# Half of an output projection, for two of four superblocks, moved beside the first four attention blocks of a hybrid decoder layer

## The reference, cut to what matters

```python
att_out = dsa_attention(q, k, v, qi, ki, wi)          # [B, T, 512]
hg_out = hgrn2_mixer(hq, hf, hi, hg, ...)             # [B, T, 512]
mix = jnp.einsum('bte,ed->btd', jnp.concatenate([att_out, hg_out], axis=-1), w_out[l])
x = x + rms_norm(mix, norm_post_mix[l])
h2 = rms_norm(x, norm_pre_ffn[l])
ff = silu(h2 @ w_gate) * (h2 @ w_up)
x = x + rms_norm(ff @ w_down, norm_post_ffn[l])
```

## Time and profile before

| | us |
|---|---|
| median of three runs | 3506.53 (3506.17 to 3509.79) |
| the profiled execution | 3509.24 |
| its span | 3507.4 |
| PE busy in the span | 3282.8 |
| VectorE busy | 2287.8 |
| ScalarE busy | 1508.7 |

### The profile page before, as it was taken

How to read it: one execution, slowest core, us unless ns; L and a number is a source line. 1 busy time by engine, 2 the same in 40 slices (tenths; PEclk the granted TensorE clock), 3 DMA queues, 4 the chain that set the end, 5 groups by cost and what they waited for, 6 DMA issues and landing times.

```text
span 3507.4 us, 46788 instructions
## 1 busy us (share of the span) xinstructions
PE 3282.8 (94%) x18176; PEld 2891.8 (82%) x18176; DVE 2287.8 (65%) x3873; ACT 1508.7 (43%) x2469; POOL 244.6 (7%) x413
## 2 busy tenths in 40 slices
PE   8989999999768899999889999998899999989998
PEld 8989999999656788888678888877788888868886
DVE  3456666888476666676777777776866765454445
ACT  3444444454354544343554444444544444333222
POOL 0000000000211100000111101010200000010000
PEclk9999999999756999999989999999999999989999
DMA  5434343343102222222421212133212121342233
GB/s 181 154 101 131 130 142 120 122 136 126 65 22 74 91 71 92 75 85 81 157 79 61 84 61 83 64 104 113 89 63 66 56 69 64 106 155 97 91 102 108
DMA packets 145389, 339.45 MB, mean 97 GB/s; under 512 B 14992, under 2 KB 35856, under 8 KB 143120
## 3 DMA queue, kind: packets, MB, share of 16 engines
q1 hardware_dynamic: 142864, 332.26, 28.4%
q10 hardware_dynamic: 2304, 4.20, 0.3%
HBM read 283.38 MB, written 53.02 MB: 96 GB/s over the span
## 4 chain that ended last, share of the span: by engine, by line
PE 63%; DVE 5%; ACT 2%; issue 2%; DMA 1%; POOL 0%; SPq 0%; DVEq 0%; ACTq 0%; POOLq 0%
PE PJ_d L1905 9%; PE PJ_d L1907 9%; PE PJ_d L1906 9%; PE SC L1868 7%; PE PJ_d L1925 6%; PE PJ_d L1927 6%; PE PJ_d L1926 6%; PE SA L1829 4%; PE SA L1830 3%; PE SA L1856 3%; PE SA L1825 1%; DVE score L1577 1%; DVE h_lo L1691 1%; DVE acc L1723 1%; DVE prob L1670 1%
## 5 line engine op out<-in xcount | busy, mean ns | idle before, releaser
L1905 PE MATMUL PJ_d<-h_hi,wd_hi 128*128 128x512 f32 (+1 forms) x1472 | 572.7, 389 | 18.7 <-DVE h_lo L1691 18.7
L1907 PE MATMUL PJ_d<-h_hi,wd_lo 128*128 128x512 f32 (+1 forms) x1472 | 562.9, 382 | 0.0
L1906 PE MATMUL PJ_d<-h_lo,wd_hi 128*128 128x512 f32 (+1 forms) x1472 | 561.8, 382 | 0.0
L1445 ACT ACTIVATE wd_hi<-wd_raw 128x512 fp32r<-128x512 f32 x592 | 358.2, 628 | 256.2 <-DMA wd_raw<-in_w_gu 147.9
L1686 DVE TENSOR_TENSOR wd_lo<-wd_raw,wd_hi 128x512 fp32r<-128x512 f32 x592 | 395.7, 690 | 64.0 <-ACT wd_hi L1445 61.1
L711 PE MATMUL PJ<-w_hi,h_hi 128*128 128x342 f32 (+1 forms) x1280 | 416.8, 326 | 6.8 <-DVE w_lo L540 6.8
L712 PE MATMUL PJ<-w_lo,h_hi 128*128 128x342 f32 (+1 forms) x1280 | 410.0, 320 | 0.0
L713 PE MATMUL PJ<-w_hi,h_lo 128*128 128x342 f32 (+1 forms) x1280 | 409.8, 320 | 0.0
L1440 ACT ACTIVATE pT<-SA 128x512 f32<-128x512 f32 (+3 forms) x320 | 156.5, 531 | 571.6 <-PE SA L1856 571.5
L1670 DVE CUSTOM_DVE_ANT_0 prob<-SA,bias 128x1024 f32<-128x1024 f32 (+7 forms) x192 | 170.2, 911 | 326.4 <-PE SA L1830 325.6
L1905 PEld LDWEIGHTS PJ_d<-h_hi,wd_hi 128*128 128x128 f32 x1472 | 278.9, 189 | 69.1 <-issue 18.8
(11 more groups left out here) (196 smaller groups left out, 5831.3 us busy)
## 6 DMA issues: line engine op xcount, KB each, us to landing
wd_raw<-in_w_gu SPq DMA_DIRECT2D x352, 256.0 KB, 3.0
wd_raw<-in_w_down SPq DMA_DIRECT2D x176, 256.0 KB, 2.6
w_raw<-in_w_in SPq DMA_DIRECT2D x40, 684.0 KB, 4.4
w_raw<-in_w_in SPq DMA_DIRECT2D x40, 676.0 KB, 4.4
row_h<-proj_d SPq DMA_DIRECT2D x16, 1024.0 KB, 7.0
wd_raw<-in_w_out SPq DMA_DIRECT2D x64, 256.0 KB, 4.1
proj_d<-stage SPq DMA_DIRECT2D x40, 342.0 KB, 4.5
proj_d<-stage SPq DMA_DIRECT2D x40, 338.0 KB, 5.3
```

The costliest lines, as they stand in the source:

```text
L1445: s_.activation(w_hi[:, u % RING, :], w_raw[:, u % RING, :], ACT.Copy).then_inc(w_hi_ready, 1)
L1905: t.matmul(to[:, tok], w_hi[:, r, w], h_hi[:, c, tok], start=(c == 0 and part != 1), stop=False)
L1906: t.matmul(to[:, tok], w_hi[:, r, w], h_lo[:, c, tok], start=False, stop=False)
L1907: last = t.matmul(to[:, tok], w_lo[:, r, w], h_hi[:, c, tok], start=False, stop=(c == KD - 1 and part != 0))
```

## The change

Superblocks 3 and 0 (`EARLY`) get two new kinds of item, placed ahead of all others and dealt over the slots from head 3 of block 0 to the indexer part of block 4: 8 `half` items transpose the recurrence's 512 columns of a tile of mixed rows (four transposes each), and 16 `part` items multiply them with rows 512 to 1023 of `w_out`, 12 matmuls each. Both superblocks use the same loaded and split weights. Superblock 0's parts stay in `acc`; those of superblock 3 are copied to `tile`, stored to `x1_d` and loaded into `acc_last` in block 15. Later, the `out` items of these two superblocks fall from 16 to 8, and their turns from 8 transposes to 4.

Other edits go with it: the first eight weight splits no longer stand together at the opening of block 2 but in the new items; six own halvings stand in place of eight for blocks of at most 512 keys; the queries are scaled by -1/8 when copied, so that the minimum on VectorE is the softmax's bias itself and `nmx` needs no instruction (in the later blocks one instruction instead of two); VectorE turns the rows of block 0 while GpSimd turns those of block 1.

```diff
+EARLY = (NS - 1, 0)
-    own_halvings = (1, 1, 1, 0, 1, 1, 1, 1, 1)
+    def own_halvings(t):
+        return (1, 0, 1, 0, 1, 1, 1, 0, 1) if NK(t) <= 2 * TOPK else (1, 1, 1, 0, 1, 1, 1, 1, 1)
-    items = [("turn", 0, i) for i in range(TS)]
+    items = [("half", s, i) for s in EARLY for i in range(TS)]
+    items += [("part", s, 1, n, i) for n in range(2) for s in EARLY for i in range(TS)]
+    PARTS = len(items)
+    items += [("turn", 0, i) for i in range(TS)]
...
-        outs = [("out", s, kg, n, i) for kg in range(2) for n in range(2) for i in range(TS)]
+        outs = [("out", s, kg, n, i) for kg in range(1 if s in EARLY else 2) for n in range(2) for i in range(TS)]
...
+        if x[0] == "part":
+            return [("part", 0, x[2], x[3], j) for j in range(4)]
...
-    loads_after, split_step = {}, {}
+    loads_after, split_step = {}, {u: 3 + u + 2 * (u // 4) for u in range(RING)}
...
+    PARTS_FROM = slots.index(("A", 0, 3))
-    for s in range(NS - 1):
+    for s in range(-1, NS - 1):
...
+        if s < 0:
+            window = window[PARTS_FROM:]
+            last = PARTS - 1
...
+            def load_halves(s):
+                to = tile[:, 0:TS, HALF_AT[s] * P:HALF_AT[s] * P + D - ATT]
+                rows = mix_d[TS * s * P:TS * (s + 1) * P, ATT:D].rearrange("(i p) e -> p i e", p=P)
+                sp.dma_start(to, rows).then_inc(half_in[s], 16)
...
+            def load_part(i):
+                t = TS * EARLY[0] + i
+                wait_pair_full(sp, ("att", NB - 1, HEADS - 1, pairs_of(NB - 1) - 1))
+                sp.dma_start(acc_last[:, i, :], x1_d[t * P:(t + 1) * P, :]).then_inc(part_in[i], 16)
...
+                if x == ("turn", EARLY[0], 0):
+                    for i in range(TS):
+                        load_part(i)
+                if x == ("part", EARLY[1], 1, 1, 2):
+                    load_mix(0, 0)
+                    load_mix(0, 1)
...
-            prep(0)
-            prep(1)
+            prep(1)
...
-                if b == 2:
-                    for u in range(RING):
-                        split_unit(u)
...
-                    s_.activation(to[0:HD, 0], heads(pair(key)[0:HD], 8), ACT.Copy)\
+                    s_.activation(to[0:HD, 0], heads(pair(key)[0:HD], 8), ACT.Copy, scale=scale)\
...
+                to = tile[:, PART_HOME[i], :] if x[0] == "part" and s == EARLY[0] else acc_of(s)[:, i, :]
...
-                wait_pair_read(dve, use[key])
                 if pairs_of(b) == 2:
-                    link(v.tensor_tensor(mxp[:, h, 0:1], mxp[:, h, 0:1], mxp[:, h, 1:2], ALU.max))
-                v.tensor_scalar(nmx[:, h:h + 1], mxp[:, h, 0:1], -SM_SCALE, None, ALU.mult).then_inc(nmx_ready, 1)
+                    wait_pair_read(dve, use[key])
+                    v.tensor_tensor(nmx[:, h:h + 1], mnp[:, h, 0:1], mnp[:, h, 1:2], ALU.min).then_inc(nmx_ready, 1)
...
+            turned_rows(v, dve, link, kept, scratch, 0)
+            v.tensor_copy(V[:, 0, :], row[:, 0, V0:V0 + KV * HD]).then_inc(row0_ready, 1)
```

More of the change, by code:

```diff
@@ L863, in mixer_phase @@
     for x in items:
-        if x[0] in ("out", "up", "down"):
+        if x[0] in ("part", "out", "up", "down"):
             done_count[x] = len(done_count) + 1
@@ L870, in read_by @@
     def read_by(x):
-        return "act" if (x[0] == "out" and x[2] == 0) or (x[0] == "down" and x[2] == 0) else "dve"
+        if x[0] == "part" or (x[0] == "out" and x[1] not in EARLY and x[2] == 0) or (x[0] == "down" and x[2] == 0):
+            return "act"
+        return "dve"
     read_count = {}
@@ L932, in mixer_phase @@
                 slot((name, b, h), head * share)
-    BESIDE = {"turn": 0.5, "gap": 0.5}
+    BESIDE = {"half": 0.5, "turn": 0.5, "gap": 0.5}
+    PARTS_FROM = slots.index(("A", 0, 3))
     fills, done = {}, 0
-    for s in range(NS - 1):
+    for s in range(-1, NS - 1):
         def first_slot(b):
@@ L1039, in mixer_phase @@
         mix_in = [sem("mix_in0"), sem("mix_in1")]
+        half_in = {s: sem(f"half_in{s}") for s in EARLY}
+        part_stored = [sem(f"part_stored{n}") for n in range(TS)]
+        part_in = [sem(f"part_in{n}") for n in range(TS)]
         x_in = [sem(f"x_in{n}") for n in range(TS)]
@@ L1218, in load_mix @@
                 sp.wait_ge(stored, 16 * (t + 1))
-                sp.dma_start(tile[:, mix_home(i), :], mix_d[t * P:(t + 1) * P, :]).then_inc(mix_in[i % 2], 16)
+                if s == 0:
+                    for n in range(TS):
+                        if PART_HOME[n] == mix_home(i):
+                            sp.wait_ge(part_stored[n], 16)
+                w = turned_width(s) * P
+                sp.dma_start(tile[:, mix_home(i), 0:w], mix_d[t * P:(t + 1) * P, 0:w]).then_inc(mix_in[i % 2], 16)
             def load_x(s, i):
                 t = TS * s + i
+                if s == 0 and X_HOME[i] in (L0, L1):
+                    sp.wait_ge(part_stored[PART_HOME.index(X_HOME[i])], 16)
                 sp.dma_start(tile[:, X_HOME[i], :], a["x"][0, t * P:(t + 1) * P, :]).then_inc(x_in[i], 16)
@@ L1476, in step @@
                 x, y = item_at(n), item_at(n - 1)
-                if y[0] in ("out", "down") and y[2] == 0:
+                if y[0] in ("part", "out", "down") and read_by(y) == "act":
                     evict(y)
@@ L1630, in topk_part @@
                         answer(t, answered.index(part) + 1)
-                    for _ in range(own_halvings[part - 1]):
+                    for _ in range(own_halvings(t)[part - 1]):
                         halve(t)
@@ L1716, in add_piece @@
                 wait_piece(dve, x)
-                wait_piece_read(dve, (kind, s, g - 1, half, i))
+                if kind == "out" and s == EARLY[0]:
+                    dve.wait_ge(part_in[i], 16)
+                elif kind == "out" and s == EARLY[1]:
+                    wait_piece_read(dve, ("part", s, 1, half, i))
+                else:
+                    wait_piece_read(dve, (kind, s, g - 1, half, i))
                 to = acc_of(s)[:, i, half * 512:(half + 1) * 512]
@@ L1750, in step @@
                 x, y, z = item_at(n), item_at(n - 1), item_at(n - 2)
[L1751 removed]
+                if y[0] in ("out", "down") and read_by(y) == "dve":
                     add_piece(y)
@@ L1777, in _ @@
             for b in range(NB):
-                if b == 2:
-                    for u in range(RING):
-                        split_unit(u)
+                if b == 1:
+                    dve.wait_ge(iota_ready, 1)
                 if b >= 1:
@@ L1870, in values, with turn @@
                     last.then_inc(pv_done, 1)
-            def turn(key, rows):
+            def turn(key, rows, width):
                 take(key)
-                for k in range(KD):
+                for k in range(width):
                     last = t.transpose(pair(key)[:, k * P:(k + 1) * P], rows[:, k * P:(k + 1) * P], ident[:])
@@ L1912, in item @@
                 tok = slice(i * P, (i + 1) * P)
-                if x[0] == "out":
-                    if g == 0 and half == 0:
+                if x[0] == "part" and half == 0:
+                    wait_pair_read(pe, use["lT", s, i])
+                if x[0] in ("part", "out"):
+                    if x[0] == "out" and g == 0 and half == 0:
                         wait_pair_read(pe, use["mT", s, i])
```

131 lines of the change are left out of this document (82 added, 49 removed).

## The result

| | before | changed |
|---|---|---|
| median | 3506.47 us | 3483.26 us (3478.59 to 3486.98, four runs) |
| ratio | | 0.9931, 95% interval 0.9919 to 0.9943 |
| profiled execution, its span | 3507.4 | 3480.1 |

What follows compares the result with a forecast made beforehand. TensorE bounds the kernel: by matmul count in blocks 5 to 7 and the tail, by half clock in blocks 0 to 3. Terms -21 - 19 - 1 - 2 + 13 + 6 - 2 = -26 us; median 3480 us, range 3452 to 3503.

Steps and rivals of the forecast that it cites:

- The sum: Whole kernel: -26 us on the profiled execution's 3509.2, so 3483, and 3480 us for a median.
- blocks 5 to 7: Blocks 5 to 7: 7 items fewer at 2.72 us, all on the path, -19 us.
- blocks 1 to 3: Blocks 1 to 3: 98.2 us of work at clock 0.80 plus 26 idle, 149 us against 143, +6.
- block 4: Block 4: one dense item more, +2.7, against narrower turns and earlier row loads, -4; -1 us (-8 to +4).
- blocks 8 to 15: Blocks 8 to 15: delayed mixed rows +2, narrower turns -3, fewer VectorE instructions 0 to -3; together -2 us.
- The tail: Tail: 8 items off the path, 21.8 us, a narrower turn -1, VectorE's additions +2; -21 us.
- My charge for VectorE's additions: Tail: VectorE instead of ScalarE handles superblock 3's first sums while finishing superblock 2, +2 us (0 to 6).
- my credit for the narrower turn: Tail: its one turn is half as wide, -1 us.
- (a): Rival in blocks 1 to 3: clock stays low, at 0.57 they take 198 us, +55, kernel 3529; 12%.
- Rival (b): Blocks 1 to 3: clock goes up and stays up, 0.95, 129 us, kernel 3460; 20%.
- Block 0: Block 0: eight halves run nearly one after the other, 8 x 2.2 us, partly hidden; +13 us (+6 to +18).
- The start: Before block 0: VectorE turns its rows in half of GpSimd's time, -2 us (-4 to 0).

Runs made afterwards that it cites:

- quads: The changed kernel with its 16 part items dealt in bursts of four instead of singly: 3507.91 us, ratio 1.0002 to the kernel before.
- dma_order: The changed kernel with superblock 0's four mixed tiles loaded early and block 15's next-turn rows ahead of the `acc_last` loads: 3475.91 us, ratio 0.9907.
- no_side_edits: The changed kernel with `nmx` by its own instruction and eight halvings again, VectorE still turning block 0's rows: 3492.2 us, ratio 0.9955.
- spare_matmuls: The kernel before, with bursts of 24 unread matmuls of 256 columns at the 14 part places of blocks 1 to 3: 3512.0 us, ratio 1.0015.

## Why the prediction was right

**The sum.** On the profiled executions -26 was forecast and -27.3 measured, on the medians 3480 and 3483.26. No term of the sum is off by more than 5.3 us, but they are off both ways (blocks 5 to 7 by 5.3, blocks 1 to 3 by 4, block 4 by 3, blocks 8 to 15 by 2), and that they cancel to 1 us is luck.

**The tail.** Forecast -21, measured -22.4: eight items at 2.72 us are 21.8, all on the path. My charge for VectorE's additions (2 us) and my credit for the narrower turn (1 us) are not seen apart.

**The clock of blocks 1 to 3.** This was the term that decides. The form, work divided by clock plus idle time, held: the work came out at 117.3 us of busy time at a mean of 0.85, which is 100 against 98.2 in the text, and the idle time at 28.5 against 26. The clock was 0.85 and not 0.80, so the blocks took 145.9 and not 149. The 0.80 was read off a list of windows in which two neighbours, 0.60 and 0.89, lie far apart; that it came so near is in part luck, and the way the clock gets there (it rises during some of the parts and stays up for the heads behind them) was not in the text. Of the rivals, (a), the clock stays low, did not happen here, but `quads` shows that it does with the same 16 items 40 us apart: 0.72 (a third of that loss is idle time and not clock), and nothing is gained. The Trainium skill, page "TensorE: Matmul & The Clock Gate", section "HAM oscillation — how this bites in real kernels", says that short bursts parted by waits start cold (at the lower clock) each time. The trace agrees for 7 of the 14 parts of blocks 1 to 3 (0.42 us apart at 977.49) and not for the other 7, whose first matmuls are already some 0.23 us apart (at 996.66), since the clock is still up from the part before. Rival (b), 0.95 and 129 us, did not happen: with 28.5 us idle even 0.95 would give 100 / 0.95 + 28.5 = 134, and with the parts doubled the clock is 0.90 and 27.4 us are still idle.

**Block 0.** +13 against +12.3. The idea of halves that run nearly one after the other for want of a third pair of banks fits the waits for `h_lo` in the timeline; no run had a third pair. What I had not weighed is where the lost time goes when they are spread: into the blocks behind it.

**Blocks 5 to 7: the step that failed.** I took seven items fewer at 2.72 us, 19 us. The list of items does have seven fewer, but three of those that left block 5 are `up` items of the first group, which have 256 columns and are half an item each. So 5.5 items' worth left, 15.0 us, and 13.7 were measured. Block 4 got the better end of the same mistake: the eight half-size items count for four, so that it holds 18 items' worth in place of 18.5, and not one more. For blocks 4 to 7 together the forecast was -20 and -17.9 was measured: the sum was nearly right and the split between them wrong.

**The rest.** The start (-1.3) and blocks 8 to 15 (0) are within the scatter of such stretches. Block 15's +2.3 is the charge that I had put at +2: the rows behind four loads; `dma_order` takes it away. Block 4's -4.2 has a wait in it that I did not foresee, 4.07 us for `tile<-mix_d`; without it 1.8 us more were gained. That I costed the missing VectorE instructions at nothing was wrong by about 5 us in blocks 1 to 3 (`no_side_edits`), and that I costed the parts' copies and splits at nothing by perhaps 7 the other way (`spare_matmuls`, with the doubt given there). Both were hidden in the chosen clock, and that they nearly cancel is luck too.

## What to carry to other kernels

In this kernel a stretch of small, waiting matmuls that ran near half clock took dense work from elsewhere for a fraction of its price, but only with the pieces one at a time and close to each other: 14 pieces of 2.7 us cost 2 to 9 us of 38, and 12 of them four at a time cost 20. Count what is moved in columns, not in items, and put the DMA that the next step waits for ahead of the large ones that can wait. When a change of the planner's weights makes one block longer, look first at what else moved into it. And when a part of the work is added to such a stretch, check each superblock's share by itself: here one half of the change, with the small edits, brought nine tenths of the gain.

## What the runs showed of the hardware

- Matmuls whose result is never read lift the granted clock: from 0.54, 0.58 and 0.60 in blocks 1 to 3 to 0.80, 0.94 and 0.89 in `spare_matmuls`. 40 us of them made the three blocks 3.2 us longer, and block 2, with five bursts in it, 2.1 us shorter (42.7 against 44.8, in one execution each).
- The clock often rises within a burst: from 0.42 us between matmuls of 512 columns (977.49) to 0.23 (980.97). In half of the 14 parts it was up from the start, and in one (1006.39) it stayed down to the end. In `quads` it was still up at the second head behind the burst (values in 0.88 us at 1068.36) and down at 1077.12 (1.54 us), with waits of 2.67 and 1.19 us between.
- The transposes and value products of a head get shorter by the clock as dense matmuls do (values 1.54 to 0.88 us), while the waits for ScalarE between them stay at 0.58; so a head gains 3.51 - 2.19 = 1.3 us.
- A wait can cost more than its length: with the 2.68 us for `tile<-mix_d` gone, block 15 is 4.3 us shorter, and the four transposes behind it take 0.63 us and not 1.04.
